# The first gate product of the second feed-forward is taken past a token tile's transposes

## What is computed

```python
def rms_norm(x, g):
    y = x * lax.rsqrt(jnp.mean(x * x, axis=-1, keepdims=True) + RMS_EPS)
    return y * g

def swiglu(h, w_gate, w_up, w_down):            # w_gate, w_up: 1024 x 4096
    return (jax.nn.silu(h @ w_gate) * (h @ w_up)) @ w_down

x = x + rms_norm(merged @ w_out, g_mix_post)    # end of the token mixing
h = rms_norm(x, g_ffn2_pre)                     # second feed-forward
x = x + 0.5 * rms_norm(swiglu(h, w_gate, w_up, w_down), g_ffn2_post)
```

## Time and profile before

| | |
|---|---|
| median of three runs | 1426.59 us (1425.34 to 1427.3) |
| the profiled execution's own time | 1426.28 us |
| its span in the profile | 1424.0 us |
| mean granted clock of PE, as a share of full speed | 0.992 |
| PE busy | 97% |
| DVE busy | 73% |
| ACT busy | 53% |
| POOL busy | 8% |

### The profile page before, as it was taken

One profiled execution on the slowest core, in us unless ns is written; L12 is line 12 of the kernel. 1 busy time (PEld: TensorE's weight loads), 2 busy tenths in 40 slices (PEclk: granted clock), 3 DMA queues, 4 the chain that ended last, 5 costly groups with the idle time before them and its releaser, 6 DMA issues.

```text
span 1424.0 us, 22721 instructions
## 1 busy us (share of the span) xinstructions
PE 1375.3 (97%) x8648; PEld 1228.2 (86%) x8648; DVE 1033.5 (73%) x1107; ACT 756.3 (53%) x1021; POOL 113.8 (8%) x164
## 2 busy tenths in 40 slices
PE   6999999999899999999989999989999999989997
PEld 6999999999688878767768888789999999977886
DVE  6977877787789864657764334687788777759896
ACT  6545444455675643657764233554454445467663
POOL 0000000002320000332320000000000000023100
PEclk9999999999999999999999999999999999999999
DMA  5323332337997653212113335232333233399974
GB/s 199 98 82 118 118 103 77 115 118 226 249 216 258 233 192 108 79 52 60 45 38 89 93 117 187 98 118 77 117 118 104 82 108 118 120 282 215 241 261 136
DMA packets 161638, 194.47 MB, mean 137 GB/s; under 512 B 6064, under 2 KB 116912, under 8 KB 161456
## 3 DMA queue, kind: packets, MB, share of 16 engines
q1 hardware_dynamic: 147808, 166.74, 35.9%
q0 software_dynamic: 13056, 25.17, 9.8%
q10 hardware_dynamic: 720, 1.84, 0.4%
HBM read 187.43 MB, written 6.29 MB: 136 GB/s over the span
## 4 chain that ended last, share of the span: by engine, by line
PE 80%; DVE 10%; DMA 5%; ACT 3%; issue 1%; POOL 1%; DVEq 0%; SPq 0%; ACTq 0%; POOLq 0%
PE ps L691 15%; PE ps L694 15%; PE ps L693 15%; PE ps L657 5%; PE ps L659 5%; PE ps L658 5%; PE ps L791 4%; PE ps L792 4%; PE ps L793 4%; DMA w_raw<-w_ffn_down 4%; DVE w_lo L1784 2%; PE ps L966 1%; PE ps L664 1%; PE ps L666 1%; PE ps L665 1%
## 5 line engine op out<-in xcount | busy, mean ns | idle before, releaser
L691 PE MATMUL ps<-s_hi,w_hi 128*128 128x256 f32 x960 | 272.6, 284 | 4.8 <-DVE w_lo L1612 4.8
L693 PE MATMUL ps<-s_lo,w_hi 128*128 128x256 f32 x960 | 272.4, 284 | 0.0
L694 PE MATMUL ps<-s_hi,w_lo 128*128 128x256 f32 x960 | 272.3, 284 | 0.0
L691 PE MATMUL ps<-a_hi,w_hi 128*128 128x256 f32 x816 | 232.0, 284 | 3.2 <-DVE a_lo L1567 3.0
L694 PE MATMUL ps<-a_hi,w_lo 128*128 128x256 f32 x816 | 231.7, 284 | 0.0
L693 PE MATMUL ps<-a_lo,w_hi 128*128 128x256 f32 x816 | 231.6, 284 | 0.0
L1154 ACT ACTIVATE w_hi<-w_sum 128x1024 fp32r<-128x1024 f32 x120 | 123.9, 1056 | 175.5 <-DVE w_sum L1639 80.4
L691 PEld LDWEIGHTS ps<-s_hi,w_hi 128*128 128x128 f32 x960 | 185.0, 193 | 5.1 <-DVE w_lo L1612 5.1
L791 PE MATMUL ps<-w_hi,l_hi 128*128 128x512 f32 x448 | 175.7, 392 | 12.1 <-DVE w_lo L1784 12.1
L693 PEld LDWEIGHTS ps<-s_lo,w_hi 128*128 128x128 f32 x960 | 185.1, 193 | 0.0
L694 PEld LDWEIGHTS ps<-s_hi,w_lo 128*128 128x128 f32 x960 | 185.0, 193 | 0.0
(11 more groups left out here) (200 smaller groups left out, 2581.6 us busy)
## 6 DMA issues: line engine op xcount, KB each, us to landing
w_raw<-w_ffn_down SPq DMA_DIRECT2D x80, 512.0 KB, 5.7
w_raw<-w_ffn_gate SPq DMA_DIRECT2D x64, 512.0 KB, 4.8
w_raw<-w_ffn_up SPq DMA_DIRECT2D x64, 512.0 KB, 5.0
d_sum<-w_ffn_down POOLq DMA_DIRECT2D x48, 512.0 KB, 10.6
w_raw<-w_in SPq DMA_DIRECT2D x44, 512.0 KB, 3.8
d_sum<-w_ffn_down SPq DMA_DIRECT2D x16, 512.0 KB, 5.7
x_mid<-x_tok SPq DMA_DIRECT2D x8, 512.0 KB, 6.0
x_tok<-x_mid SPq DMA_DIRECT2D x8, 512.0 KB, 7.2
```

What stands on the lines that cost most here:

```text
L691: pe.matmul(o, wh, hi[:, k, :], start=first and f == 0 and k == 0, stop=False, skip_group_check=True)
L693: pe.matmul(o, wh, lo[:, k, :], start=False, stop=False, skip_group_check=True)
L694: mm = pe.matmul(o, wl, hi[:, k, :], start=False, stop=last and k == KH - 1, skip_group_check=True)
```

## The change

On PE, in the second feed-forward, the call `first_gate(1, U_UP2, 0, 0)` stands in front of `transposed(2, 2)` and no longer behind it. Nothing else differs.

```diff
             last_out(3, (0,))
             transposed(2, 1)
             last_out(3, (1,))
+            first_gate(1, U_UP2, 0, 0)
             transposed(2, 2)
-            first_gate(1, U_UP2, 0, 0)
             first_gate(1, U_UP2, 0, 1)
             first_up(1, U_UP2, 0, 0)
             transposed(2, 3)
```

## The result

The changed kernel took 1429.68 us, the median of 20 runs (1426.49 to 1432.49), against 1426.71 us for the kernel before (20 runs, 1422.33 to 1429.65). The ratio is 1.0025, with a 95% interval of 1.0017 to 1.0032. That is 3.0 us by the medians and 3.6 us by the ratio. The forecast was 1428.3, 1.67 us slower, and 0.86 of the chance was laid on less than 0.2%. The change is slower, and by the ratio it is slower by more than that, a case that had been given 0.11; the interval begins at 0.17%, so that it is more than 0.2% is likely and not certain. 1429.68 lies inside the range, which reached to 1429.9 for the sake of a rival, the two low stretches at the gate, that did not come about.

What follows compares the result with a forecast made beforehand. PE, busy 97% of the span, was taken as the bound. Gate product 0, uncovered transposes 0.87 and clock 0.8 summed to 1.67 us, added to 1426.59 for 1428.3 us; range 1426.0 to 1429.9.

Steps and rivals of the forecast that it cites:

- the two low stretches at the gate: Rival: clock falls at the moved gate product and stays low for two stretches; 3.9 us slower, 1430.5 us, chance 0.08.
- The gate product gains nothing: At the moved gate product: its own operand, tile 1's remainder, comes at 923.66 in either order; gain taken as 0.
- The transposes cost 0.87 us: Behind the gate product: tile 2's eight transposes no longer fill idle time and lengthen PE's stream by 0.87 us.
- The bound of 1.20 from the first feed-forward: Other bound for the eight transposes' cost, read at their copy behind the same gate product in the first feed-forward: 1.20 us.
- Nobody waits for tile 2: After tile 2's transposes: ACT reads them at 929.86, when they would be done already; cost 0.
- The cover of 0.8 us: Time left between tile 2's transposes ending at 929.1 with the slow clock and ACT reading them at 929.86.
- The delay leaves PE at tile 3's transposes and is passed on: At tile 3's transposes: ACT and DVE were idle for them, so PE's start at 957.6 comes later by about as much.
- The 0.5 us of slack on DVE: DVE's idle time in 23 us before PE's start at 957.6; if some absorbed the delay, 0.4 us would be left.
- The clock costs 0.8 us: At the gate product: 3.2 us of idle time may halve the clock; middle of 0 and 1.51 us taken.
- The twin in the first feed-forward: Same gate product in the first feed-forward, behind 2.98 us idle: low clock, 4.44 us against 2.93, so 1.51 us.
- "A part comes back" at the restart: Behind PE's 3.7 us wait: a later start puts some low clock onto idle time; as a rival up to 1.5 us, chance 0.06.
- the same: Whole kernel: measured time within 0.2%, 2.85 us, of before, so 1423.74 to 1429.44; chance 0.86.

Runs made afterwards that it cites:

- e1: Kernel before, with tile 2's transposes run twice: in the idle time ahead of the gate product and again behind it; ratio to before 1.0009.
- e3: Changed kernel with twelve matmuls nobody reads put into the idle time ahead of the gate product; ratio to before 1.0015.
- e9: Changed kernel with five unread matmuls at the end of the idle time, right in front of the gate product; ratio to before 1.0009.
- e11: Kernel before with ten unread matmuls, 2.3 us, in front of tile 3's transposes; ratio to before 1.0023.
- e2: Changed kernel with seven of tile 2's eight transposes left out; ratio to before 1.0029.
- e5: Changed kernel run once more, with nothing altered, beside another group of kernels; ratio to before 1.0019.
- e7: Changed kernel with fourteen unread matmuls in PE's 3.7 us wait ahead of product 6; ratio to before 0.9993.
- f2: Rerun in a later group: changed kernel with fourteen unread matmuls in PE's 3.7 us wait; ratio to before 1.0000.
- e8: Changed kernel with five unread matmuls at the start of the idle time, 2.05 us left idle right ahead of the gate product; ratio to before 1.0016.
- e10: Changed kernel with five unread matmuls right in front of the gate product and fourteen in the 3.7 us wait; ratio to before 0.9993.
- e6: Kernel before with fourteen unread matmuls in PE's 3.7 us wait ahead of product 6; ratio to before 0.9975.
- f1: Rerun in a later group: kernel before with fourteen unread matmuls in PE's 3.7 us wait; ratio to before 0.9988.
- e12: Kernel before with unread matmuls in two places: fourteen in the 3.7 us wait, twelve ahead of the first feed-forward's first gate product; ratio to before 0.9975.
- f3: Kernel before with tile 2's transposes run both ahead of and behind the gate product, and unread matmuls in the 3.7 us wait; ratio to before 0.9998.
- f4: Rerun in a later group: changed kernel with five unread matmuls before the gate product and fourteen in the 3.7 us wait; ratio to before 0.9987.

## Why the prediction was wrong in size and right in mechanism

- **The gate product gains nothing.** Right: it starts 2.52 us behind tile 2's normalising, as before. What was moved in front had been waiting for something else.
- **The transposes cost 0.87 us.** Right, measured 0.86 to 0.88 in the segments. The bound of 1.20 from the first feed-forward was not needed. The whole times of the kernels with nothing but this term (e1, e3, e9) lie at 1.2 to 1.7 us above before, each with an interval that holds 0.87.
- **Nobody waits for tile 2.** Right: ACT took it up without a wait even behind the slow gate. The cover of 0.8 us that the prediction had left for this case sufficed (transposes started at 930.08, ACT at 931.77).
- **The delay leaves PE at tile 3's transposes and is passed on.** Right: 2.36 us there and 2.36 at the restart; e11 confirms it with 2.29 for 2.3. The 0.5 us of slack on DVE took up nothing.
- **The clock costs 0.8 us.** This is the step that failed, on both of its sides. Its upper end at the gate, 1.51, was the size itself: among the five profiles with the whole hole open (after, e2, e5, e7, f2) the clock fell in four, each time 1.0 to 1.2 us behind the gate's start, so that the slow stretch lay wholly on work, and cost 1.48. Taking the middle for "the clock need not fall in all" halved a term that occurred in most of the profiles. The twin in the first feed-forward had shown it at full price, and it took 4.19 us or more in all seventeen profiles in which its hole is open. (In eight of them the clock's records begin only behind its start, so they don't show whether the clock fell there or had not yet risen.)
- **"A part comes back" at the restart.** The sign was wrong. In both profiles of the changed kernel the low time on work behind the restart was 5.8 us in place of 3.4, and cost 1.0 us more. e8, which had a fall at the gate and the changed kernel's full delay, shows it as well (6.8 us low); e2, with a fall and less delay, and e11, with the delay and no fall, do not. So it was seen with the two together, three times out of three. The profiles show how the two go together. From the fall at the gate to the fall at the restart are 34.1 us in all four profiles that have both (after, e2, e5, e8). In the three with the full delay PE restarts 0.95 to 1.03 us behind that second fall, and the low stretch is 6.8 us long; in e2 it restarts 0.2 us behind it and in e11 0.5, and the stretch is 3.4. It was the same in the down stage of e10: 1.4 us, and 6.8. That this holds in general is not shown, and the whole times don't confirm it, since e6 and e7 gained nearly the same by closing the place. The prediction had looked at the shift of the restart, and expected that more idle time under the low clock would give time back.
- **The sum.** 0.88 + 1.48 + 1.0 = 3.4 us, against 3.6 by the first ratio and 2.7 by that of e5. The mean clock says the same from many executions: 0.9915 in 20 and in 12 runs of the changed kernel, 0.9935 to 0.9940 in those of before. That is 0.0020 to 0.0025 of 1428 us, twice over since the clock halves: 6 to 7 us more at 1.2 GHz, or 2.5 to 3.1 us lost at 44%. With 0.88 it makes 3.4 to 4.0. The gate's term is shown by the segments; the 1.0 at the restart is an estimate from three profiles.
- **The rival of two low stretches.** It had the time nearly right (3.9 us) and the place wrong: two in a row came at the restart, not at the gate, where one stretch brought the clock back every time.
- **The chances.** Part of the 0.86 for "the same" followed from the 0.8 us. With the twin's 1.51 in full, the sum would have been 2.4 us. From there to 2.85, where the prediction set its bound for 0.2%, are 0.5 us, less than the restart's term.

A shorter kernel came out of the experiments: the kernel before, with fourteen matmuls that nobody reads in the 3.7 us ahead of the restart (e6 and f1), at 0.9975 and 0.9988 of its time. The interval of f1 reaches to 1.0000, that of e6 only to 0.9985.

## What to carry to other kernels

Look at what an instruction waits for before putting it in front of another: if its own operand comes at the same time in any order, whatever it is put in front of loses its place in a hole. Price a hole on TensorE twice, as the time in it and as the clock behind it, and take the clock's term from the same pattern elsewhere in the trace at full size. But ask first what PE waits for shortly behind it, as e12 shows. And when a difference is near the scatter of whole executions, read a segment from the last common event to the first one that all must pass; it gave 0.02 us here where the ratio gave 1.5.

## What the runs showed of the hardware that was not expected

- The length of a hole does not tell whether the clock falls. 2.05 us right in front of the gate were followed by a fall (e8, one profile); 2.00 to 2.02 us with 1.1 to 1.3 us of transposes or matmuls between them and the gate were not, in ten of ten (before, e1, e6, e9 to e12, f1, f3, f4). In the kernel before it fell at 627.7 us too, 1.7 us behind the end of a hole of only 1.35 us. Whether the place of the idle time or chance makes the difference is open.
- The same hole of 3.18 to 3.19 us was followed by a fall in four profiles and by none in a fifth (f2). Between the start-up and the end of the span, low stretches lasted 3.4 us or 6.8 us.
- A low clock need not cost time: with its hole filled the first gate product took 2.88 us in place of 4.19 or more (e12), and a later wait for a weight remainder took the gain up.
- Matmuls whose result nobody reads made a kernel faster: fourteen of 128x512, 3.4 us of work in a hole, saved 3.6 us on one chip and 1.8 on another.
- The part before the change ran for 917.9 us (f3) to 923.5 us (e8) up to tile 2's normalising, on the same code (e12 is left out here, since it has a filler there). Two profiles of the changed and the unchanged kernel differed by 4.9 us in span, and 1.9 of them lay there.
